# RMS scales of the mixing, memory, cross and expert norms applied behind the projections they feed

## The chip, the cores and the metric

The kernel runs as one program on one core of a Trainium2 chip. The metric is the device time of the whole program in microseconds (us). Engines are named as in the profile: PE multiplies matrices (PEld is its weight load), DVE is the vector engine, ACT the scalar engine, POOL the GpSimd engine, SP issues the DMA stream of weights.

## The reference, cut to what matters

Two blocks follow each other over 256 tokens of width 2048, stored transposed as x[128 partitions, 16 feature blocks k, 256 tokens]. The first ends with a final norm; the second has four norms whose outputs feed projections:

```
x = rmsnorm(x, final_norm_w)                       # "f1", end of the first block
h = rms_norm(x, g_mix);  proj = h @ w_in           # "mix": rq rk rv rg | dq dk dv | two gates
ret = retention(rotate(rq), rotate(rk), rv);  ret = ret * silu(rg)
dil = dilated_attention(rotary(dq), rotary(dk), dv)
x = x + (sigmoid(gate_ret)*(ret @ w_br_ret) + sigmoid(gate_dil)*(dil @ w_br_dil)) @ w_out
hc = rms_norm(x, g_cross);  memn = rms_norm(mem, g_mem)
x = x + memory_cross_attention(hc, memn, w_q, w_kv, w_o)
hf = rms_norm(x, g_ffn);  x = x + peer_ffn(hf, w_q, subkeys, u_tab, v_tab)
# rms_norm(x, g) = x * r * g, r = rsqrt(mean(x*x over features) + 1e-6), one r per token
```

Since r is one number per token, (x * g * r) @ W = ((x * g) @ W) * r.

## The kernel before, in words

**A tile of weights.** All weight matrices pass as tiles of 128 outputs by 2048 inputs through a ring of four buffers, loaded by SP's queue. For each half of a tile ACT rounds it into w_hi (line 1123), POOL subtracts to get the remainder w_lo (line 414), and PE multiplies: with w_hi 8 matmuls of 512 columns, the activations' rounded and remainder parts side by side (line 453), and with w_lo 8 of 256 columns (line 455). w_hi and w_lo have four half-tile slots, so ACT rounds a half once PE has finished the half four before it. DVE adds the two halves of the psum bank into the output tile (line 1545 in copy stages, 1980 where it is added to x). There are four banks, and four ring buffers. In index n of a stage's loop ACT thus works two tiles ahead of PE, POOL right behind ACT, and DVE when PE has finished tile n.

**Stages around the change**, in tiles: mlp (8 rounds of 8 up tiles, whose squared-relu result "hid" DVE splits at lines 2014 to 2018, and 8 down tiles, added to x at line 2025), ret 32, dil 36, gate 32, br_ret 8, br_dil 4 (merged with the sigmoid gates at lines 2185 to 2191), out2 16, kv 32 (16 for K, 16 for V), q 16, o 16, pq 16 (the experts' query, with key scores, and the top 16 of each half of the keys on DVE), then up and down tiles of the experts.

**A norm** stands between two stages. ACT squares x in quarters of four blocks into ntmp (line 1150), DVE sums them over the blocks in halves (line 1501, norm_part), PE sums over the partitions with two matmuls by ones (line 479), DVE forms mean+eps, ACT takes the root (line 1154), DVE the reciprocal, and then quarter by quarter DVE multiplies x by gain and r into ntmp (line 1537), ACT rounds to the high part (line 1162), DVE subtracts to get the low part (line 1528). The stage's first matmul waits for the first quarter. "f1" and "mix" run one after the other behind mlp, followed by the sine tables of the rotations (lines 2037 to 2047); "mem" runs behind br_dil, ahead of out2; "cross" behind the 16th kv tile; "ffn" behind o. The order on each engine is the order in which its program is written; semaphores join them.

## Time and profile before

| | |
|---|---|
| median of three runs | 4832.02 us (4825.33 to 4833.13) |
| span of the profiled execution | 4820.5 us |
| PE busy in the span | 4398.7 us (91%), 24530 matmuls |
| DVE / ACT / POOL busy | 2616.8 (54%) / 1728.6 (36%) / 3284.8 us (68%) |

The profile gives the profiled execution only as its span, the time from its first to its last instruction, without a time of its own; the three timed runs lie 4.8 to 12.6 us above that span, which is what lies around it. Read the table as: one engine, PE, is nearly always busy; what counts is where it is not.

### The profile page before, as it was taken

The page shows a single profiled execution, that of the slowest core. Times are in us where ns is not written, and L with a number is a line of the kernel's source. Part 1 is how long each engine was busy: PE and PEld are TensorE (multiplying, and loading weights), DVE is VectorE, ACT ScalarE, POOL GpSimd, SP SyncE. Part 2 cuts the span into 40 slices and gives each one's busy share as a digit, 9 for nine tenths or more (in the row PEclk, how much of TensorE's full clock was granted, in tenths as well). Part 3 has the DMA queues.
Part 4 walks back from the last instruction along what each step waited for, and adds up shares of the span by engine and source line. Part 5 has one row for each costly group of instructions (what it writes and reads, how often), then busy time and mean ns, then how long its engine had stood idle before and what let it go on. Part 6 is the DMA issues. An engine that isn't in the chain of part 4 may idle for free.

```text
span 4820.5 us, 66241 instructions
## 1 busy us (share of the span) xinstructions
PE 4398.7 (91%) x24530; PEld 3674.6 (76%) x24530; DVE 2616.8 (54%) x3800; ACT 1728.6 (36%) x1827; POOL 3284.8 (68%) x1304
## 2 busy tenths in 40 slices
PE   8898987899999969996988898898899999999998
PEld 1677754688888858885877786788888788888886
DVE  3325765355455553314163312496976886795794
ACT  1234422333333333432534432443333333333333
POOL 0357730678888847872867784677687788788776
PEclk9999979899999979997999999999999999999999
DMA  8356740345455534551544452444354454445443
GB/s 312 115 196 253 293 158 35 139 165 184 178 182 182 182 112 158 182 181 59 186 156 157 157 189 97 149 149 148 139 191 170 163 189 179 166 175 180 170 171 125
DMA packets 111085, 804.56 MB, mean 167 GB/s; under 512 B 12903, under 2 KB 13192, under 8 KB 14088
## 3 DMA queue, kind: packets, MB, share of 16 engines
q1 hardware_dynamic: 108720, 787.30, 45.0%
q10 hardware_dynamic: 2200, 14.90, 0.9%
q8 instruction: 122, 2.00, 0.2%
q14 instruction: 43, 0.35, 0.0%
HBM read 800.06 MB, written 2.10 MB: 166 GB/s over the span
## 4 chain that ended last, share of the span: by engine, by line
POOL 31%; PE 30%; issue 24%; DVE 4%; POOLq 1%; ACT 0%; DMA 0%; DVEq 0%; ACTq 0%
POOL w_lo L414 31%; PE psum L453 16%; PE psum L455 8%; PE psum L550 1%; DVE out_hl L2364 1%; PE psum L442 1%; PE psum L443 1%; PE psum L444 1%; PE psum L1071 1%; DVE out_hl L2362 1%; DVE hid L2360 0%; POOLq L411 0%; DVE mix_m L1789 0%; PE psum L1042 0%; DVE mix_t L1789 0%
## 5 line engine op out<-in xcount | busy, mean ns | idle before, releaser
L414 POOL TENSOR_TENSOR w_lo<-ring,w_hi 128x1024 fp32r<-128x1024 f32 x1240 | 3010.3, 2432 | 1389.2 <-ACT w_hi L1123 1388.7
L1123 ACT ACTIVATE w_hi<-ring 128x1024 fp32r<-128x1024 f32 x1240 | 1309.5, 1060 | 2173.5 <-PE psum L455 1939.6
L453 PE MATMUL psum<-hc_hl,w_hi 128*128 128x512 f32 x5440 | 1945.9, 401 | 109.5 <-DVE hc_hl L1528 43.7
L455 PE MATMUL psum<-hc_hl,w_lo 128*128 128x256 f32 x5440 | 1529.2, 281 | 0.0
L453 PEld LDWEIGHTS psum<-hc_hl,w_hi 128*128 128x128 f32 x5440 | 1029.6, 189 | 360.5 <-issue 71.6
L455 PEld LDWEIGHTS psum<-hc_hl,w_lo 128*128 128x128 f32 x5440 | 1036.2, 190 | 2.0 <-issue 1.9
L453 PE MATMUL psum<-out_hl,w_hi 128*128 128x512 f32 x2048 | 728.3, 400 | 26.3 <-issue 14.1
L455 PE MATMUL psum<-out_hl,w_lo 128*128 128x256 f32 x2048 | 577.1, 282 | 0.0
L453 PEld LDWEIGHTS psum<-out_hl,w_hi 128*128 128x128 f32 x2048 | 388.8, 190 | 123.3 <-issue 21.6
L455 PEld LDWEIGHTS psum<-out_hl,w_lo 128*128 128x128 f32 x2048 | 391.2, 191 | 0.0
L453 PE MATMUL psum<-hid_hl,w_hi 128*128 128x512 f32 x1024 | 360.9, 398 | 14.0 <-DVE hid_hl L2018 14.0
L429 POOL TENSOR_TENSOR ada_acc<-ada_acc,ada_row 128x2048 f32<-128x2048 f32 x56 | 256.2, 4575 | 70.3 <-ACT ada_row L1220 64.8
L455 PE MATMUL psum<-hid_hl,w_lo 128*128 128x256 f32 x1024 | 286.1, 279 | 0.0
L2025 DVE SCALAR_TENSOR_TENSOR x<-psum,mod,x 128x256 f32<-128x256 f32 x256 | 124.0, 484 | 227.3 <-PE psum L455 222.7
L550 PE MATMUL psum<-x,ring 128*128 128x256 f32 x1024 | 234.0, 389 | 8.4 <-DMA ring<-mixed 5.2
L453 PEld LDWEIGHTS psum<-hid_hl,w_hi 128*128 128x128 f32 x1024 | 192.3, 188 | 62.9 <-DVE hid_hl L2018 16.5
L550 PEld LDWEIGHTS psum<-x,ring 128*128 128x128 f32 x1024 | 197.6, 195 | 45.9 <-DMA ring<-mixed 7.9
L2372 DVE TENSOR_TENSOR x<-psum,x 128x256 f32<-128x256 f32 x256 | 107.9, 421 | 203.1 <-PE psum L455 196.9
L2364 DVE TENSOR_TENSOR out_hl<-hid,out_hl 128x256 fp32r<-128x256 f32 x128 | 197.9, 1546 | 4.4
L455 PEld LDWEIGHTS psum<-hid_hl,w_lo 128*128 128x128 f32 x1024 | 193.0, 188 | 0.0
L453 PE MATMUL psum<-mem_hl,w_hi 128*128 128x512 f32 x512 | 184.1, 404 | 9.6 <-POOL w_lo L414 9.6
L2016 DVE CAST hid_hl<-hid 128x256 fp32r<-128x256 f32 x64 | 159.8, 2497 | 2.2
(386 smaller groups left out, 5178.9 us busy)
## 6 DMA issues: line engine op xcount, KB each, us to landing
ring<-stream SPq DMA_DIRECT2D x652, 1024.0 KB, 4.8
ring<-mixed SPq DMA_DIRECT2D x96, 1024.0 KB, 6.5
x<-x ACTq DMA_DIRECT2D x2, 2048.0 KB, 11.2
ctx_raw<-ctx ACTq DMA_DIRECT2D x1, 2048.0 KB, 9.8
mem_raw<-mem ACTq DMA_DIRECT2D x1, 2048.0 KB, 7.6
out<-x SPq DMA_DIRECT2D x4, 512.0 KB, 2.6
filt_w<-filt_w ACTq DMA_DIRECT2D x1, 1024.0 KB, 11.0
dft<-dft ACTq DMA_DIRECT2D x1, 1024.0 KB, 12.7
```

Of the source, the lines that this page charges most:

```text
L414: pool.tensor_tensor(w_lo[:, slot], ring[:, s, k], w_hi[:, slot].bitcast(F32), ALU.subtract).then_inc(lo_ready, 1)
L429: pool.tensor_tensor(ada_acc[:, n % 2], ada_row[:, 0] if k == 1 else ada_acc[:, n % 2], ada_row[:, k % 2], ALU.add).then_inc(ada_done, 2 i ...
L442: pe.matmul(o, w_hi[:, slot, c], x_hi, start=start(c), stop=False)
L443: pe.matmul(o, w_hi[:, slot, c], x_lo, start=False, stop=False)
L453: pe.matmul(psum[:, b, :].rearrange("p (s t) -> p s t", s=2), w_hi[:, slot, c], x_hl, start=start(c), stop=False, skip_group_check=True)
L455: m = pe.matmul(psum[:, b, 0:T], w_lo[:, slot, c], x_hl[:, 0], start=False, stop=stop(c), skip_group_check=True)
L550: m = pe.matmul(psum[:, (3, 7)[i % 2], 0:T], ring[:, (3 * i) % RING, k], x[:, k], start=k == 0, stop=k == KC - 1)
L1123: act.activation(w_hi[:, 2 * (s % 2) + h], ring[:, s, k], ACT.Copy).then_inc(hi_ready, 1)
L2016: dve.tensor_copy(hid_hi[:, j], s).then_inc(dve_step, 1)
L2025: dve.scalar_tensor_tensor(x[:, d], psum[:, 4 + d % 4, s * T:s * T + T], mod[:, gate + d, 0:1], x[:, d], ALU.mult, ALU.add).then_inc(acc_f ...
L2364: dve.tensor_tensor(out_lo[:, j], hid[:], out_hi[:, j].bitcast(F32), ALU.subtract).then_inc(hid_ready, 1)
L2372: st.did(dve.tensor_tensor(x[:, d], psum[:, 4 + d % 4, 0:T], x[:, d], ALU.add))
```

## The change

It keeps every product and every norm, and moves where r is applied. The activations that a projection reads are now x * gain without r, rounded (ACT) and subtracted (DVE, `gained_low`) quarter by quarter inside the loop of the stage before. The squares and their sums run inside a tile loop too. r itself is made later and applied to what comes out: for ret to the rotation tables, to V on its way to natural order, and to the silu gate's input; the gate tiles are multiplied by it one by one (32); the K half of kv tile by tile (16), the V half at its turn; for cross in the scale of the softmax's Exp; for pq in that of the chosen scores' Exp. A row of r (r_row) serves where tokens lie along the free axis, a column (r_col) where they are partitions. The experts' up tiles still read the true h, which ACT and POOL make again during pq. The final norm of block one multiplies x during ret tiles 9 to 16. The sine tables are computed inside the last mlp round. Parts of the diff, cut to what the next section speaks of:

```diff
+            pool.wait_ge(xg_made, q + 1)
+            pool.tensor_tensor(ntmp[:, q % 2], ntmp[:, q % 2], r_row[:].unsqueeze(1).broadcast_to([P, 4, T]),
+                               ALU.mult).then_inc(xg_scaled, 1)
...
+            pool.tensor_tensor(h_lo[:, 4 * q:4 * q + 4], ntmp[:, q % 2], h_hi[:, 4 * q:4 * q + 4].bitcast(F32),
+                               ALU.subtract).then_inc(hn_lo, 1)
...
+        for n in range(8, KC):
+            g, s = FIRST["pq"] + n, n % RING
...
+            if n == 9:
+                pool.wait_ge(r_made, FFN_MADE)
+            if n in (10, 11, 13, 14):
+                ffn_scale((10, 11, 13, 14).index(n))
+            if n in (12, 13, 15):
+                ffn_low((12, 13, 15).index(n))
+        ffn_low(3)
+        split(2 * EXPERT_B, 2 * (FIRST["peer"] - SPLIT0))
...
+            def moving(k):
+                if after is not None and n == 0 and k % 4 == 0:
+                    pe.wait_ge(norm_lo, 4 * NS[after] + k // 4 + 1)
+                return hl[:, :, k]
+            for h in range(2):
+                half_wide(FIRST[name] + n, n % RING, h, lambda c: h == 0 and c == 0,
+                          lambda c: h == 1 and c == KC // 2 - 1, lambda c: n % RING, lambda c: moving(h * 8 + c))
...
+            if n == 2:
+                norm_pe("f1")
+            if n == 5:
+                norm_pe("mix", 5, mix_part)
+            if n == 7:
+                turn_root(1)
+            if n in (8, 9, 10, 11):
...
+        for n in range(KC):
+            tile("out2", n, h_hl)
+            if n == 12:
+                norm_pe("mem", column=True)
+        for n in range(KC):
+            tile("kv", n, mem_hl[:], "mem")
+            if n == 13:
+                norm_pe("cross", row=False, column=True)
...
+        def ffn_squares(q):
+            pe.wait_ge(norm_sq, 4 * NI["ffn"] + q + 1)
+            for k in range(4):
+                m = pe.matmul(psum[:, 7, 0:T], sq(ONES), ntmp[:, q % 2, k], start=q + k == 0, stop=q + k == 6)
+            m.then_inc(sq_used, 1)
...
+            act.wait_ge(acc_free, 4 + n_acc["peer"] - KC + 4 * q + 4)
+            gained(q, x, lambda k: final_mix[:, k:k + 1], h_hi)
...
+        act.dma_start(pos_i[:], a["pos"]).then_inc(s_aux, 16)
...
+                trig_sines(0)
+            if j == 9:
+                trig_sines(1)
+                act.wait_ge(r_made, FM_MADE)
+            if j in (12, 14):
+                mix_gained((j - 12) // 2)
+        split_at(FIRST["ret"])
+        mix_gained(2)
+        split_half(FIRST["ret"] + 1, 1, 0, True)
+        mix_gained(3)
+        split_half(FIRST["ret"] + 1, 1, 1)
+        square("f1", x, 0)
+        square("f1", x, 1)
+        def mix_square(q):
+            act.wait_ge(norm_half, 2 * NH["mix"] if q < 2 else 2 * NH["mix"] + 1)
+            for k in range(4):
+                m = act.activation(ntmp[:, q % 2, k], x[:, 4 * q + k], ACT.Square, scale=col("final1", 4 * q + k))
+            m.then_inc(norm_sq, 1)
...
+                square("f1", x, 3)
+            if n in (3, 4):
+                mix_square(2 * n - 6)
+                mix_square(2 * n - 5)
+            if n == 5:
+                root("f1")
+            if n == 8:
+                root("mix")
...
+            q = k // 4
+            m = act.activation(hi[:, k], src[:, k], ACT.Copy, scale=col(name, k))
+            if k % 4 == 3:
+                m.then_inc(norm_hi, 1)
+            if k % 8 == 0:
+                act.wait_ge(norm_half, 2 * NH[name] + k // 8)
+            m = act.activation(ntmp[:, q % 2, k % 4], src[:, k], ACT.Square)
+            if k % 4 == 3:
+                m.then_inc(norm_sq, 1)
+        for n in range(KC):
+            split_at(FIRST["out2"] + n)
+            if n == 2:
+                act.wait_ge(merged, 1)
+            if 2 <= n < 10:
...
+            split_at(FIRST["kv"] + n)
+            if n == 2:
+                act.wait_ge(bank_free, 4 + bank_of["kv"])
+            if 2 <= n < 10:
+                gained_squared("cross", x, h_hi, 2 * n - 4)
...
+        def ffn_again(q):
+            act.wait_ge(sq_used, 4)
+            if q >= 2:
+                act.wait_ge(hn_lo, q - 1)
+            for k in range(4):
+                m = act.activation(ntmp[:, q % 2, k], x[:, 4 * q + k], ACT.Copy, scale=col("ffn", 4 * q + k))
+            m.then_inc(xg_made, 1)
...
+        def ffn_high(q):
+            act.wait_ge(xg_scaled, q + 1)
+            act.activation(h_hi[:, 4 * q:4 * q + 4], ntmp[:, q % 2], ACT.Copy).then_inc(hn_hi, 1)
...
+        for n in range(KC):
+            split_at(FIRST["o"] + n)
+            if n in (6, 10, 14):
+                ffn_gained((n - 6) // 4)
+        split_at(FIRST["pq"])
+        split_half(FIRST["pq"] + 1, 1, 0, True)
+        ffn_gained(3)
+        split_half(FIRST["pq"] + 1, 1, 1)
...
+            if n < 6:
+                ffn_square(n - 2)
+            if n == 8:
+                root("ffn")
+            if n in (9, 10):
+                ffn_again(n - 9)
+            if n in (12, 13):
+                ffn_high(n - 12)
+            if n in (14, 15):
+                ffn_again(n - 12)
+            if n in (15, 16):
+                ffn_high(n - 13)
...
-        up_down_dve(FIRST["mlp"], bank_of["mlp"], 0, HID0, dict(STREAM)["mlp"] // 16, 5 * KC)
-        norm_dve("f1", x, lambda k: col("final1", k), plain=x)
-        dve.wait_ge(plain_done, 2 + 4)
-        norm_dve("mix", x, lambda k: col("mix", k))
...
+                m = dve.scalar_tensor_tensor(lo[:, k], src[:, k], gain(k), hi[:, k].bitcast(F32), ALU.mult, ALU.subtract)
+            m.then_inc(norm_lo, 1)
...
+                if d == 0:
+                    trig_cosine(0)
+                    trig_angle(1)
+                if d == 6:
+                    trig_cosine(1)
+                if d in (7, 11):
+                    dve.wait_ge(acc_free, 4 + acc0 + d + 1)
+                    mix_low((d - 7) // 4)
+                if d == 14:
+                    mix_low(2)
...
+        dve.wait_ge(acc_free, 4 + n_acc["peer"])
+        mix_low(3)
...
+        norm_half_sum("f1", 0)
         for n in range(RET_TILES):
             evict("ret", n, pr[:, n])
-            if n in (4, 5, 8, 9):
-                ret_v((n // 4 - 1) * 2 + n % 2)
+            if n == 0:
+                norm_half_sum("f1", 1)
+            if n == 2:
...
+                norm_half_sum("mix", 0, mix_part)
+            if n == 3:
+                dve.wait_ge(norm_rt, NI["f1"] + 1)
+                st.did(dve.reciprocal(nrstd[:], nrt[:]))
+                st.settle()
+                st.did(dve.tensor_tensor(nrt[:], nrstd[:], nrstd[:], ALU.mult))
+                norm_half_sum("mix", 1, mix_part)
+            if n == 5:
...
+                st.did(dve.scalar_tensor_tensor(nrt[:], psum[:, 5, 0:T], 1.0 / D, nrt[:], ALU.mult, ALU.mult))
+                st.settle()
+                dve.tensor_scalar(nrt[:], nrt[:], EPS, None, ALU.add).then_inc(norm_ms, 1)
...
+                st.did(dve.reciprocal(r_row[:], nrt[:]))
+                st.settle()
+                dve.tensor_tensor(r_row[:], r_row[:], nrstd[:], ALU.mult).then_inc(r_made, 1)
...
+            if n == 7:
+                st.settle()
+                st.did(dve.tensor_tensor(trig[:], trig[:], r_row[:].unsqueeze(1).broadcast_to([P, 4, T]), ALU.mult))
+                root_column(1, MIX)
...
+            if 9 <= n < 17:
+                for k in (2 * n - 18, 2 * n - 17):
+                    m = dve.scalar_tensor_tensor(x[:, k], x[:, k], col("final1", k), nrstd[:], ALU.mult, ALU.mult)
...
+        dve.wait_ge(bank_free, 4 + bank_of["dil"])
+        dve.tensor_tensor(pr[:, 24:32], pr[:, 24:32], r_row[:].unsqueeze(1).broadcast_to([P, 8, T]),
+                          ALU.mult).then_inc(pg_scaled, 1)
...
+                both(blk, j).then_inc(bank_free, 1)
+                dve.wait_ge(bank_free, i * RING + (4 + bank_of["gate"] + j + 1))
+                dve.tensor_tensor(blk, blk, r_row[:], ALU.mult).then_inc(pg_scaled, 1)
...
+            dve.wait_ge(half_done, 2 * (FIRST[name] + n) + 2)
+            st.did(dve.tensor_tensor(x[:, n], psum[:, n % RING, 0:T], x[:, n], ALU.add))
+            st.settle()
+            dve.tensor_tensor(x[:, n], psum[:, n % RING, T:], x[:, n], ALU.add).then_inc(bank_free, 1)
+        for n in range(KC):
+            added("out2", n)
+            if n in (3, 5, 7, 9):
+                gained_low("mem", (n - 3) // 2, mem_raw, lambda k: col("mem", k), mem_hi, mem_lo)
+            if n in (6, 10):
+                norm_half_sum("mem", (n - 6) // 4)
...
+        st.did(dve.reciprocal(r_row[:], nrt[:]))
...
+            st.did(dve.tensor_tensor(kv[:, n], kv[:, n], r_row[:], ALU.mult))
+            if n in (3, 5, 7, 9):
+                gained_low("cross", (n - 3) // 2, x, lambda k: col("cross", k), h_hi, h_lo)
+            if n in (6, 10):
+                norm_half_sum("cross", (n - 6) // 4)
+            if n == 13:
...
+        for n in range(KC):
+            added("o", n)
+            if n in (7, 11, 14):
+                ffn_low_part((n - 7) // 4 if n < 14 else 2)
         dve.wait_ge(bank_free, 4 + bank_of["pq"])
-        norm_dve("ffn", x, lambda k: col("ffn", k), summed=1)
+        ffn_low_part(3)
...
-            both(q_peer[:, n], n % RING).then_inc(bank_free, 1)
+            if n >= RING:
+                dve.wait_ge(p_sc, n - RING + 1)
+            both(q_peer[:, n % RING], n % RING).then_inc(bank_free, 1)
...
+                dve.wait_ge(sq_used, 4)
+                dve.tensor_scalar(nrt[:], psum[:, 7, 0:T], 1.0 / D, EPS, ALU.mult, ALU.add).then_inc(norm_ms, 1)
```

On ACT, between the last br_dil split and the first out2 tiles, before:

```order
L1150 ACTIVATE ntmp<-mem_raw 128x1024 x4
L1123 ACTIVATE w_hi<-ring 128x1024 x2
L1154 ACT_TABLE_LOAD
L1154 ACTIVATE nrt<-nrt 128x256
L1123 ACTIVATE w_hi<-ring 128x1024 x2
L1162 ACTIVATE mem_hl<-ntmp,cols 128x256 x16
L1123 ACTIVATE w_hi<-ring 128x1024 x4
```

The same piece of ACT after, from one out2 tile (L1187 is the split of a tile) to its two blocks of the memory norm:

```order
L1187 ACTIVATE w_hi<-ring 128x1024 x2
L1530 ACTIVATE mem_hl<-mem_raw,cols 128x256
L1535 ACTIVATE ntmp<-mem_raw 128x256
L1530 ACTIVATE mem_hl<-mem_raw,cols 128x256
L1535 ACTIVATE ntmp<-mem_raw 128x256
```

The norm's squares and high parts moved from a block of their own into the tile loop, two blocks of x behind each of eight splits (out2 tiles 2 to 9, in index n). The kv loop has the same form.

On DVE in the out2 loop, after, from tile 5 to tile 7 (L2486 and L2488 add a psum bank to x, L1687 is the half sum of the squares, L2220 the low parts):

```order
L2486 TENSOR_TENSOR x<-psum,x 128x256
L2488 TENSOR_TENSOR x<-psum,x 128x256
L2220 SCALAR_TENSOR_TENSOR mem_hl<-mem_raw,cols,mem_hl 128x256 x4
L2486 TENSOR_TENSOR x<-psum,x 128x256
L2488 TENSOR_TENSOR x<-psum,x 128x256
L1687 TENSOR_REDUCE norm_part<-ntmp 128x256
L2486 TENSOR_TENSOR x<-psum,x 128x256
L2488 TENSOR_TENSOR x<-psum,x 128x256
L2220 SCALAR_TENSOR_TENSOR mem_hl<-mem_raw,cols,mem_hl 128x256 x4
```

Each such row now stands behind the adds of a tile, while before all of them stood in front of the first.

On POOL in the pq stage, after (L461 splits half a tile, L430 multiplies four blocks by r, L437 makes their low parts):

```order
L461 TENSOR_TENSOR w_lo<-ring,w_hi 128x1024 x6
L430 TENSOR_TENSOR ntmp<-ntmp,r_row 128x1024
L461 TENSOR_TENSOR w_lo<-ring,w_hi 128x1024 x2
L430 TENSOR_TENSOR ntmp<-ntmp,r_row 128x1024
L461 TENSOR_TENSOR w_lo<-ring,w_hi 128x1024 x2
L437 TENSOR_TENSOR hc_hl<-ntmp,hc_hl 128x1024
L461 TENSOR_TENSOR w_lo<-ring,w_hi 128x1024 x2
L430 TENSOR_TENSOR ntmp<-ntmp,r_row 128x1024
L437 TENSOR_TENSOR hc_hl<-ntmp,hc_hl 128x1024
L461 TENSOR_TENSOR w_lo<-ring,w_hi 128x1024 x2
L430 TENSOR_TENSOR ntmp<-ntmp,r_row 128x1024
L461 TENSOR_TENSOR w_lo<-ring,w_hi 128x1024 x2
```

Before, nothing but splits stood there; eight instructions of another kind are new.

## Rows read from the trace of the kernel before

**Rows 1.** busy time, clock and DMA of the four norms' stretches
```profile
core 0: us, PE busy (x) PEld busy (x) DVE busy (x) ACT busy (x) POOL busy (x), PEclk, DMA share, GB/s
1703.30:1777.40 74.10, 27.45 (x110) 20.52 (x110) 51.89 (x82) 27.73 (x41) 20.46 (x9) 0.65 0.17 59
2526.50:2568.60 42.10, 25.18 (x107) 20.98 (x108) 30.58 (x43) 20.06 (x30) 21.66 (x9) 0.70 0.24 83
2731.50:2767.50 36.00, 22.48 (x108) 18.92 (x106) 27.08 (x39) 14.74 (x25) 19.54 (x9) 0.81 0.27 91
3082.60:3114.00 31.40, 10.31 (x42) 7.26 (x41) 26.03 (x38) 14.91 (x25) 11.97 (x5) 0.73 0.19 67
```

**Rows 2.** what PE waited for, 1703.3 to 1777.4 (us, times, longest)
```profile
PE psum L479 <- DVE norm_part L1501: 28.7, 4, 12.8
```

**Rows 3.** DVE in time, both norms behind mlp (start, us, [idle before])
```profile
1703.46 1.00 DVE L2025 SCALAR_TENSOR_TENSOR x<-psum,mod,x 128x256 f32<-128x256 f32 x2 [1.77 <-PE psum L455]
1706.53 3.59 DVE L1501 TENSOR_REDUCE norm_part<-ntmp 128x256 f32<-128x2048 f32 x1 [2.07 <-ACT ntmp L1150]
...
1776.70 0.69 DVE L1545 TENSOR_REDUCE pr<-psum 128x256 f32<-128x512 f32 x1 [9.32 <-PE psum L455]
1782.25 0.69 DVE L1545 TENSOR_REDUCE pr<-psum 128x256 f32<-128x512 f32 x1 [4.86 <-PE psum L455]
```

**Rows 4.** DVE in time, last eviction before and first behind mem, cross, ffn
```profile
2526.08 0.43 DVE L2191 TENSOR_TENSOR hc_hl<-mrg,hc_hl 128x256 fp32r<-128x256 f32 x1
...
2567.72 0.88 DVE L1980 TENSOR_TENSOR x<-psum,x 128x256 f32 x2 [7.03 <-PE psum L455]
...
2731.55 0.69 DVE L1545 TENSOR_REDUCE kv<-psum 128x256 f32<-128x512 f32 x1 [3.87 <-PE psum L455]
...
2766.76 0.69 DVE L1545 TENSOR_REDUCE kv<-psum 128x512 f32 x1 [6.54 <-PE psum L455]
...
3082.66 0.88 DVE L1980 TENSOR_TENSOR x<-psum,x 128x256 f32<-128x256 f32 x2 [3.46 <-PE psum L455]
...
3113.29 0.69 DVE L1545 TENSOR_REDUCE q_peer<-psum 128x256 f32<-128x512 f32 x1 [1.77 <-PE psum L455]
```

**Rows 5.** groups by line, 2600 to 2720, an undisturbed stretch of tiles
```profile
L414 POOL TENSOR_TENSOR w_lo<-ring,w_hi 128x1024 fp32r<-128x1024 f32 x43 | 103.1, 2397 | 18.5 <-ACT w_hi L1123 18.5
L1123 ACT ACTIVATE w_hi<-ring 128x1024 fp32r<-128x1024 f32 x42 | 44.6, 1062 | 74.1 <-PE psum L455 74.1
```

**Rows 6.** ACT in time, high parts of the mix norm
```profile
1744.80 3.30 ACT L1162 ACTIVATE hc_hl<-ntmp,cols 128x256 fp32r<-128x256 f32 x8 [5.06 <-DVE ntmp L1537]
```

**Rows 7.** DVE and POOL in time: mlp round, then br_dil with and without POOL
```profile
1619.31 2.51 DVE L2016 CAST hid_hl<-hid 128x256 fp32r<-128x256 f32 x1
1619.27 2.41 POOL L414 TENSOR_TENSOR w_lo<-ring,w_hi 128x1024 fp32r<-128x1024 f32 x1 [0.37 <-ACT w_hi L1123]
2501.39 2.21 DVE L2187 TENSOR_TENSOR mrg<-mrg,pg 128x256 f32<-128x256 f32 x1
2509.94 0.42 DVE L2187 TENSOR_TENSOR mrg<-mrg,pg 128x256 f32<-128x256 f32 x1
```

**Rows 8.** PE in time behind a long wait
```profile
2992.30 0.79 PE L453 MATMUL psum<-hc_hl,w_hi 128*128 128x512 f32 x1 [6.53 <-POOL w_lo L414]
```

**Rows 9.** busy time in the pq stage and in the first up tiles
```profile
3114.00:3206.00 92.00, 90.49 (x531) 78.46 (x530) 81.45 (x346) 35.22 (x44) 71.47 (x30) 1.00 0.45 164
3230.00:3300.00 70.00, 65.34 (x536) 64.33 (x535) 44.89 (x14) 32.31 (x38) 68.87 (x23) 1.00 0.46 165
```

**Rows 10.** what PE waited for, 3114 to 3314
```profile
PE psum L1010 <- DVE q_peer L1545: 7.4, 6, 5.9
```

**Rows 11.** from the page: groups by line (busy, mean ns | idle before, releaser)
```profile
L453 PE MATMUL psum<-hc_hl,w_hi 128*128 128x512 f32 x5440 | 1945.9, 401 | 109.5 <-DVE hc_hl L1528 43.7
...
L453 PE MATMUL psum<-hid_hl,w_hi 128*128 128x512 f32 x1024 | 360.9, 398 | 14.0 <-DVE hid_hl L2018 14.0
...
L550 PE MATMUL psum<-x,ring 128*128 128x256 f32 x1024 | 234.0, 389 | 8.4 <-DMA ring<-mixed 5.2
```

More of the change, by code:

```diff
@@ L1137, in split_stage, with square, root, gained @@
                     split_tile(i * RING + (g0 + s), i + g0 // RING, s)
+        def square(name, src, q):
+            if q >= 2:
+                act.wait_ge(norm_half, 2 * NH[name] + 1)
+            act.activation(ntmp[:, q % 2], src[:, 4 * q:4 * q + 4], ACT.Square).then_inc(norm_sq, 1)
+        def root(name):
+            act.wait_ge(norm_ms, NI[name] + 1)
+            act.activation(nrt[:], nrt[:], ACT.Sqrt).then_inc(norm_rt, 1)
+        def gained(q, src, gain, hi):
+            for k in range(4 * q, 4 * q + 4):
+                m = act.activation(hi[:, k], src[:, k], ACT.Copy, scale=gain(k))
+            m.then_inc(norm_hi, 1)
         def norm_act(name, src, shift=None, split=True, ready=None, ahead=None):
@@ L1147, in norm_act @@
                     act.wait_ge(*ready(q))
[L1148 to L1150 removed]
+                square(name, src, q)
             if ahead is not None:
@@ L1482, in _ @@
         act.wait_ge(p_cv, 1)
-        act.activation(chosen[:, 2], chosen[:, 2], ACT.Exp).then_inc(p_ge, 1)
+        for tb in range(2):
+            m = act.activation(chosen[:, 2, tb], chosen[:, 2, tb], ACT.Exp, scale=r_col[:, FFN, tb:tb + 1])
+        m.then_inc(p_ge, 1)
         up_act(0, EARLY, QUARTER - EARLY)
```

311 lines of the change are left out of this document (204 added, 107 removed).

## The prediction, made before the changed kernel ran

> **What bounds the kernel now.** I read the page first: PE is busy 91% of the span and its 512-column matmuls cost 0.401 us each, so what can be won is PE's idle time. The page puts 109.5 us of idle before one group of matmuls, most of it behind line 1528, the last step of a norm [rows 11]. Then I read busy time by stretches for the places where a norm stands between two stages: PE is busy only 27.45 of 74.1 us, 25.18 of 42.1, 22.48 of 36.0 and 10.31 of 31.4, with a granted clock of 0.65 to 0.81, while elsewhere it is 1.00 [rows 1, 9]. In the first stretch the waits name the half sums alone with 28.7 us [rows 2]: PE does not wait for one slow instruction but for a chain of ACT, DVE, PE, DVE, ACT, DVE.
>
> What each norm costs I take from the evictions on DVE, because one follows each finished tile. A tile takes 1782.25 − 1776.70 = 5.55 us. Behind mlp the last add to x starts at 1703.46 and the third ret tile is evicted at 1776.70: 73.24 − 3 × 5.55 = **56.6 us** lost to f1 and mix [rows 3]. In the same way [rows 4]: from the last merged block, 2526.08, to out2 tile 2, 2567.72, 41.64 − 16.65 = **25.0** (mem); from kv tile 15, 2731.55, to kv tile 18, 2766.76, 35.21 − 16.65 = **18.6** (cross); from o tile 15, 3082.66, to pq tile 0, 3113.29, 30.63 − 5.55 = **25.1** (ffn). In all 125.3 us. This is the most that the change can give back, lower clock behind the waits included; the matmuls of the projections are the same in number and shape.
>
> **The change part by part.** What is removed is the four waits, −125.3. What it puts in their place:
>
> *Mix.* The low parts of the first three quarters are written behind mlp's down tiles 3, 5 and 7. The fourth can't start before the last add to x: the adds 1.00 [rows 3], four high parts on ACT at 3.30/8 = 0.41 each [rows 6], four low parts on DVE at 0.42 to 2.4. PE has three quarters of a tile (4.2 us) to do meanwhile, but one half split must also be made between; I take 4. Further on, ACT and DVE now make the sums and roots in the tile loop. Each place where ACT waits for DVE holds up its next split: ACT's squares of the mixed x (index 5) behind DVE's half sum of 3.59 [rows 3], the two roots with their table loads, the sines in the last mlp round. PE's own small matmuls and the transposes of the root add a little. I take 5 for these and 3 for the 16 multiplications of x by the final gain, which stand in front of the retention's steps and share memory with POOL. Together 12, between 4 (all hidden but the last quarter) and 25 (each late by a POOL instruction).
>
> *Silu input and gates.* 32 multiplications by r, one per gate tile, 0.42 to 2.4 each beside 0.69 of eviction in 5.55 us: hidden. At the end br_ret waits for the last, and for one wide multiplication ahead of the silu: 3 (0 to 6).
>
> *Mem.* In br_dil DVE merges blocks at 2 instructions of 0.42 and a cast and a subtraction; while POOL splits, one of these took 2.21 [rows 7]. Before, POOL had nothing to do there, since out2's splits stood behind the norm. Now ACT and POOL split out2 tiles 0 and 1 during the merge: four POOL instructions, each of which may hold DVE by 2.21 − 0.42 = 1.8, so up to 7.2. PE waits for the merge at this point; I take 6.5. PE then starts behind a wait, and a 512-column matmul behind one of 6.53 us took 0.79 in place of 0.40 [rows 8, 11]: 1.3 more. Sum 7.8 (2 to 12).
>
> *The two stalls in out2 and kv.* In index 6 ACT wants to square block 8 into the buffer of the first half and waits for DVE's half sum. That sum stands behind the adds of tile 6, and these wait for PE to finish tile 6. ACT's split of tile 7 stands behind the square. So when PE has finished tile 6, tile 7 isn't split: adds or eviction 0.9, sum 3.59, one or two squares and a high part 1.2, half a split 1.06 on ACT, 2.40 on POOL [rows 3 to 5], that is 9.1, plus hand-overs, 9.4; and 1.2 for the clock. 10.6 for each of out2 and kv, **21.2**. The same doesn't come again in index 10, where ACT has no square left that waits. Bounds 0 and 30.
>
> *Cross otherwise.* Sixteen multiplications of K by r, the low parts, and the scale in Exp lie beside the tiles: 0 (0 to 6).
>
> *Ffn.* The fourth quarter as in mix, but with short adds: 0.8. PE sums the squares over partitions by itself, 16 matmuls of 256 f32 columns at 0.389 [rows 11]: 6.2, not hidden, for PE is the busy engine. POOL gets eight instructions over four blocks of x, the size of a half split: 8 × 2.40 = 19.2 in tiles 10 to 15 [rows 5]. In the pq stage it is busy 71.47 of 92.0 us [rows 9], that is 20.5 free over 15 tiles (30 splits), 1.37 each; over six tiles 8.2, so 11 are left over and POOL, which PE waits for, is late by them. ACT takes 8 rounds more, but is at 35.22 of 92.0. Behind pq the up tiles leave POOL no slack at all (68.87 of 70.0 [rows 9]), so that nothing is won back there, and a start without lead costs some 3. On the other side PE waited 5.9 at the end of pq for the last query tile, behind DVE's top-16 work [rows 10], and lost 1.2 to the clock behind it; with PE late, DVE has caught up. 0.8 + 6.2 + 11 + 3 − 7.1 = 13.9 (5 to 25).
>
> Sum: −125.3 + 12 + 3 + 7.8 + 21.2 + 13.9 = −67.4 us. On the span of 4820.5 that is 4753; the median lies 11.5 above the span, so **4765 us**.
>
> A rule speaks against the change. By the trace, an SBUF cast of DVE that started while POOL split took 2.51 us, to the end of POOL's instruction, and a product of two SBUF tiles 2.21 against 0.42 alone [rows 7]. The Trainium skill, "SBUF — State Buffer", section "Who interferes with whom", says that a VectorE instruction of the kind with two SBUF inputs and a GpSimd one that reads SBUF exclude each other, each keeping the shared port for its whole instruction. The trace agrees. By that rule every low part moved into a loop where POOL is at work costs more than where POOL rested; where DVE's lead covers it the sum stays at −67, at full price it is rival A.
>
> **The rivals.**
>
> A: *slower, by that exclusion.* The change puts 128 DVE instructions over two SBUF tiles into loops in which POOL splits: 64 low parts, 16 products of K, 32 of the gates, 16 of x. If each delays PE by a whole POOL instruction, 128 × 2.40 = 307, less 125.3, is +182: 5014 us. It decides from 125.3/128 = 1.0 us each. Against it: in mlp each of 64 up tiles has three such steps with POOL at work, and all PE idle behind them is 14.0 us [rows 11], 0.2 per tile. DVE has three banks of lead. 3%.
>
> B: *better: nearly everything hides.* If in index 6 ACT had enough lead, or POOL's extra work in pq fell into slack, 21 or 11 to 14 us of the sum go: 4744 for the first, about 4730 for both, and at the very best 4832 − 118 = 4714. For it: ACT idles 74 of 120 us in such a loop [rows 5]. Against it: the wait in index 6 is one of order, not of load. 20%.
>
> C: *less: moved waits cost more.* Bursts of four low parts beside POOL delay evictions by over three banks, POOL's lateness in pq runs on, and mix comes to its upper bound: 25 + 6 + 12 + 30 + 25 = 98 given back, −27: 4805. For it: all but the matmul terms rest on single instructions. 13%.
>
> D: *it doesn't shorten*, because the weights would bound PE in place of the norm. The DMA share is 0.17 to 0.27 in these stretches and 0.45 in pq [rows 1, 9], far from full. 1%.
>
> **How the numbers follow.** Forecast 63%, with its own range 4747 to 4782; A 3%, B 20%, C 13%, D 1%. Some 0.2% (10 us) is what a measurement of this kernel tells from no change. Within it lie D and the far end of C: 2%. Slower 3%. Faster 95%. For 8 in 10 I leave out the better half of B, the far half of C, A and D: 4735 to 4800.
>
> **What would show it.** Right: no stretch of DVE's evictions behind mlp, br_dil, kv tile 15 and o over 15 us; PE waiting about 10 us for POOL's split of tile 7 in out2 and in kv; PE waits for splits in pq tiles 11 to 15, about 11 us; the merge in br_dil with casts or products of over 2 us; last wait of pq gone. Wrong: no wait at tile 7 (B), a clock of 1.00 in pq throughout (B), or waits for evictions spread over every tile of the loops (A, C).

## The result, and the profile after

The changed kernel takes 4777.23 us (median of 4 runs, 4768.23 to 4782.63) against 4828.68 of the kernel before beside it (4 runs, 4824.33 to 4833.13): a ratio of 0.9902, 95% interval 0.9886 to 0.9919, some 51 us less by the medians and 47 by the ratio. The forecast was 4765, with a range of 4735 to 4800. The profiled execution has a span of 4773.0 us against 4820.5, 47.5 us less.

The head of the page after:

```profile
span 4773.0 us, 66080 instructions
...
PE 4410.6 (92%) x24574; PEld 3687.1 (77%) x24574; DVE 2683.7 (56%) x3793; ACT 1744.9 (37%) x1885; POOL 3311.5 (69%) x1312
```

Busy time of the stretches that answer to [rows 1], in the same columns: from the last add of mlp to the third ret tile; the merge in br_dil; from its end to the third out2 tile; from the last o tile to the first pq tile; and the pq stage, for [rows 9]:

```profile
1708.10:1728.80 20.70, 16.28 (x84) 13.86 (x83) 13.11 (x10) 14.79 (x22) 12.50 (x6) 0.92 0.32 110
2449.40:2492.90 43.50, 26.70 (x167) 24.97 (x165) 41.28 (x64) 8.40 (x8) 19.98 (x9) 0.80 0.34 117
2492.90:2511.40 18.50, 18.50 (x97) 16.25 (x98) 1.70 (x4) 8.13 (x13) 11.21 (x5) 0.91 0.21 74
3032.50:3041.90 9.40, 6.04 (x27) 5.00 (x26) 4.88 (x6) 4.29 (x7) 5.07 (x2) 0.85 0.36 115
3041.20:3160.60 119.40, 103.70 (x574) 90.21 (x573) 100.89 (x370) 52.86 (x72) 92.10 (x39) 0.94 0.38 132
```

The norms' holes are closed. Between the same starts as in [rows 3, 4], 73.2 us behind mlp became 21.2, 41.6 behind the merge 19.0, 35.2 behind kv tile 15 became 16.8, and 30.6 behind o 9.1. What came in their place stands in the waits of PE (us, times, longest), the view to read next. Its first row is of the whole execution, the second of the pq stage; of the seven waits in the first row one of 6.6, at the head of o, was there before with 6.5:

```profile
PE psum L492 <- POOL w_lo L424: 31.7, 7, 9.4
...
PE psum L1068 <- DVE q_peer L1731: 11.7, 4, 6.8
```

The account by stages comes from the evictions on DVE, as in the prediction, for both profiled executions (length of each stretch in us, from start to start; where a tile is added to x in two steps, the second; the kernels of the experiments are cut at the same evictions):

| stretch, up to | before | after | difference | forecast |
|---|---|---|---|---|
| first up tile of the last mlp round | 1618.1 | 1610.0 | -8.2 | 0 |
| last add of mlp | 85.9 | 98.2 | +12.3 | with ret |
| last ret tile | 257.2 | 209.4 | -47.8 | -44.6 with mlp |
| first merged block of br_dil | 530.6 | 531.8 | +1.2 | +3 |
| last merged block | 34.3 | 43.0 | +8.7 | +6.5 |
| last out2 tile | 115.5 | 105.2 | -10.3 | -13.1 |
| last kv tile | 198.6 | 190.8 | -7.8 | -8.0 |
| last o tile | 243.0 | 244.2 | +1.2 | 0 |
| first pq tile | 30.2 | 8.7 | -21.5 | -24.3 |
| last pq tile | 98.7 | 118.7 | +20.0 | +17.2 |
| end | 1608.5 | 1613.1 | +4.6 | -4.1 |

Two of these rows, the first and the last, hold no changed work that explains them. Up to the last mlp round the program is nearly the same, and the changed kernels below reached it between 1606.8 and 1619.4 us; in the stretch from the last pq tile to the end they took 1605.8 to 1616.8. So stretches of the same code differ by up to 13 us between executions. Single effects are read below from the length of their own stage, and the yardstick for each is how far kernels with the same code in it lie apart: the last mlp round took 95.0 to 98.4 us, the merge in br_dil 41.1 to 43.0, and pq 117.1 to 118.7. Each stage is read in one execution per kernel.

### The profile page after: what moved, and what is told of

Its sections match the earlier page's. It is cut to its first block, busy times and chain, and to the rows that moved or that the text cites. A ratio compares the mean times of both kernels' runs of the same rounds, so it can differ in the third digit from the quotient of the medians.

```text
span 4773.0 us, 66080 instructions
## 1 busy us (share of the span) xinstructions
PE 4410.6 (92%) x24574; PEld 3687.1 (77%) x24574; DVE 2683.7 (56%) x3793; ACT 1744.9 (37%) x1885; POOL 3311.5 (69%) x1312
## 4 chain that ended last, share of the span: by engine, by line
PE 33%; POOL 29%; issue 21%; DVE 5%; POOLq 0%; ACT 0%; DMA 0%; DVEq 0%; ACTq 0%
POOL w_lo L424 28%; PE psum L492 18%; PE psum L494 9%; PE psum L607 1%; DVE out_hl L2698 1%; PE psum L481 1%; PE psum L482 1%; PE psum L483 1%; PE psum L1132 1%; DVE out_hl L2696 1%; POOL w_lo L461 1%; DVE hid L2694 0%; DVE mix_m L1976 0%; POOLq L421 0%; PE psum L1103 0%
## 5 line engine op out<-in xcount | busy, mean ns | idle before, releaser
L424 POOL TENSOR_TENSOR w_lo<-ring,w_hi 128x1024 fp32r<-128x1024 f32 x1224 | 2979.9, 2440 | 1309.1 <-ACT w_hi L1187 1308.5
L1187 ACT ACTIVATE w_hi<-ring 128x1024 fp32r<-128x1024 f32 x1240 | 1309.9, 1060 | 2151.7 <-PE psum L494 1899.8
L492 PE MATMUL psum<-hc_hl,w_hi 128*128 128x512 f32 x5184 | 1853.0, 401 | 86.4 <-DVE hc_hl L2151 24.5
L494 PE MATMUL psum<-hc_hl,w_lo 128*128 128x256 f32 x5184 | 1455.0, 281 | 0.0
L492 PEld LDWEIGHTS psum<-hc_hl,w_hi 128*128 128x128 f32 x5184 | 980.3, 189 | 327.3 <-issue 47.9
L494 PEld LDWEIGHTS psum<-hc_hl,w_lo 128*128 128x128 f32 x5184 | 985.0, 190 | 2.0 <-issue 1.9
L492 PE MATMUL psum<-hid_hl,w_hi 128*128 128x512 f32 x1024 | 366.7, 402 | 20.4 <-DVE hid_hl L2205 12.3
L2212 DVE SCALAR_TENSOR_TENSOR x<-psum,mod,x 128x256 f32<-128x256 f32 x224 | 108.5, 484 | 201.7 <-PE psum L494 197.7
L481 PE MATMUL psum<-hc_hl,w_hi 128*128 128x256 f32 x512 | 150.8, 294 | 5.3 <-POOL w_lo L424 5.3
## 6 DMA issues: line engine op xcount, KB each, us to landing
filt_w<-filt_w ACTq DMA_DIRECT2D x1, 1024.0 KB, 10.6
```

Source lines behind the costliest of these rows:

```text
L424: pool.tensor_tensor(w_lo[:, slot], ring[:, s, k], w_hi[:, slot].bitcast(F32), ALU.subtract).then_inc(lo_ready, 1)
L481: pe.matmul(o, w_hi[:, slot, c], x_hi, start=start(c), stop=False)
L492: pe.matmul(psum[:, b, :].rearrange("p (s t) -> p s t", s=2), w_hi[:, slot, c], x_hl, start=start(c), stop=False, skip_group_check=True)
L494: m = pe.matmul(psum[:, b, 0:T], w_lo[:, slot, c], x_hl[:, 0], start=False, stop=stop(c), skip_group_check=True)
L1187: act.activation(w_hi[:, 2 * (s % 2) + h], ring[:, s, k], ACT.Copy).then_inc(hi_ready, 1)
L2212: dve.scalar_tensor_tensor(x[:, d], psum[:, 4 + d % 4, s * T:s * T + T], mod[:, gate + d, 0:1], x[:, d], ALU.mult, ALU.add).then_inc(acc_f ...
```

## The experiments

All are edits of the changed kernel. A ratio is to the kernel before, measured beside it, with its 95% interval. The medians of the kernel before lay between 4821.2 and 4828.7 us, so kernels of different groups are compared more safely by their ratios than by their medians.

### Where the half sum stands

```diff
-            if n in (6, 10):
-                norm_half_sum("mem", (n - 6) // 4)
+            if n in (4, 10):
+                norm_half_sum("mem", n // 10)
```

The same for "cross".

> From the changed kernel, DVE's first half sum of the squares stands behind tile 4 of out2 and of kv in place of tile 6. Theory (a wait of order): ACT's split of tile 7 no longer waits for PE to finish tile 6, the two steps between evictions of 17.1 and 17.0 us fall to the pitch of 5.6, PE's waits of 9.1 and 9.4 us for POOL's split go: 22 us less than the changed kernel's 4777, so 4755. Rival (a matter of load: DVE's low parts, held up by POOL, use up the lead): the stall only moves to another tile, less than 10 us are won, 4767 or more.

Measured 4750.95 us, ratio 0.9848 (0.9832 to 0.9864), 26 us under the changed kernel, whose interval (0.9886 to 0.9919) lies above. The stall in the changed kernel can be read link by link. DVE: tiles 6 and 7 of out2, with the half sum between; ACT: its square of block 8 waits for that sum, and the split of tile 7 stands behind it; POOL waits for ACT:

```profile
2533.59 0.42 DVE L2486 TENSOR_TENSOR x<-psum,x 128x256 f32<-128x256 f32 x1 [3.08 <-PE psum L494]
2534.05 0.42 DVE L2488 TENSOR_TENSOR x<-psum,x 128x256 f32<-128x256 f32 x1
2534.39 3.58 DVE L1687 TENSOR_REDUCE norm_part<-ntmp 128x256 f32<-128x2048 f32 x1
2550.71 0.42 DVE L2486 TENSOR_TENSOR x<-psum,x 128x256 f32<-128x256 f32 x1 [12.73 <-PE psum L494]
```

```profile
2538.01 0.42 ACT L1535 ACTIVATE ntmp<-mem_raw 128x256 f32<-128x256 f32 x1 [14.05 <-DVE norm_part L1687]
...
2539.04 1.99 ACT L1187 ACTIVATE w_hi<-ring 128x1024 fp32r<-128x1024 f32 x2
```

```profile
2540.15 14.31 POOL L424 TENSOR_TENSOR w_lo<-ring,w_hi 128x1024 fp32r<-128x1024 f32 x6 [14.11 <-ACT w_hi L1187]
```

With the sum behind tile 4, ACT waits 4.25 us at the same place, PE has no wait in out2, and one of 1.5 us in kv (its waits there, the whole answer):

```profile
PE psum L492 <- POOL w_lo L424: 1.5, 1, 1.5
```

out2 took 86.9 us from first to last tile in place of 97.2, kv 183.1 in place of 190.8: 18.0 together, under the 22 expected. The step into tile 7 fell from 17.1 to 5.7 us and from 17.0 to 7.4, 21.0 together; the other tiles took 3.0 more, with DVE's low parts held up by POOL. The medians differ by 8 us more than that; between the profiled executions, 7 us lie in the stretch behind pq, where nothing was changed. The wait was one of order, not of load.

### POOL's eight instructions in pq

```diff
-            pool.tensor_tensor(ntmp[:, q % 2], ntmp[:, q % 2], r_row[:]. ...
+            pool.tensor_tensor(ntmp[:, q % 2, :, 0:4], ntmp[:, q % 2, :, 0:4], ...
```

> From the changed kernel, POOL's eight instructions that make the experts' input again in pq work on 4 of the 256 tokens; the rest of that input is left out. Theory of the forecast (POOL is overloaded by 8 x 2.4 = 19.2 us, of which 11 show): 11 to 14 us less, 4764. Rival (pq is bound by DVE, which PE waits for 11.7 us there against 4.0 for POOL): at most 5 us less, 4772.

Measured 4775.71 us, ratio 0.9906 (0.9889 to 0.9922). The pq stage took 114.9 us in place of 118.7: 3.8 us, not 11 (2.2 against the shortest stage of the same code). POOL was no longer late (PE waited 0.5 us for it), and PE's waits for DVE's query tile grew from 11.7 to 13.6. The forecast's mechanism for pq falls.

### The expert norm as a block again

The norm stands between o and pq as before, without the squares on PE and the work on ACT and POOL in pq (some 60 lines back to their old form, in the new buffers).

> From the changed kernel, the expert norm alone goes back to what it was before: a block between o and pq, PE without the 16 matmuls over squares, POOL without the eight instructions. The forecast's sum (this part gives 11.2 us): 4788. Rival, read from the two traces (from the last q tile to the end the changed kernel is 6.0 us longer than the kernel before): 6 us less than the changed kernel, 4771.

Measured 4788.52 us, ratio 0.9922 (0.9904 to 0.9940); the intervals of this and of the changed kernel overlap, so the 11 us between the medians are not shown, though the median came where the forecast's sum had put it. The traces do not carry them: from the first o tile to the last pq tile it took 214.8 us, the changed kernel 213.7 (84.7 + 31.5 + 98.6 against 86.3 + 8.7 + 118.7). 7 of the 15 us between the spans lie in the memory attention, whose code is the same, at a granted clock of 0.78 against 0.88 (70 us each, this kernel first):

```profile
2885.00:2955.00 70.00, 48.45 (x185) 37.88 (x185) 20.56 (x33) 12.79 (x24) 5.05 (x3) 0.78 0.04 16
```

```profile
2877.00:2947.00 70.00, 48.64 (x215) 39.01 (x215) 21.29 (x35) 14.62 (x26) 11.72 (x5) 0.88 0.10 34
```

So this part of the change is worth about 1 us by its stages, in one execution of each; by the times alone 11 us cannot be ruled out. What it takes out of the hole between o and pq it gives back inside pq.

### out2's first splits behind the merge

```diff
         for n in range(KC):
-            split_at(FIRST["out2"] + n)
-            if n == 2:
+            if n == 0:
                 act.wait_ge(merged, 1)
+            split_at(FIRST["out2"] + n)
```

> From the changed kernel, ACT splits out2's tiles 0 and 1 only when the merge of br_dil is done, so that POOL rests in the merge's second half. Theory (DVE and POOL exclude each other: four merge steps took 2.35 to 2.59 us in place of 0.29 to 0.43): merge 8.5 us shorter, then 1.06 + 2.40 us of split ahead of PE: 5 us less, 4772. Rival (the merge is bound by PE or its own length): 3.5 us more, 4781.

Measured 4773.96 us, ratio 0.9893 (0.9877 to 0.9910), too little to tell from the changed kernel by time. By stage both terms came as the theory had them: the merge took 34.6 us in place of 43.0 (8.4 less; 6.5 against the shortest merge of the same code), and from its end to the first out2 tile 11.7 in place of 8.0 (3.7 more). In the changed kernel, one merge step that POOL held and what POOL did then:

```profile
2479.39 2.35 DVE L2474 CAST hc_hl<-mrg 128x256 fp32r<-128x256 f32 x1
2481.78 0.43 DVE L2476 TENSOR_TENSOR hc_hl<-mrg,hc_hl 128x256 fp32r<-128x256 f32 x1
```

```profile
2479.06 2.54 POOL L424 TENSOR_TENSOR w_lo<-ring,w_hi 128x1024 fp32r<-128x1024 f32 x1 [1.22 <-ACT w_hi L1187]
```

The cast starts inside POOL's instruction and ends 0.14 us behind it, at 2481.7; alone it takes 0.29. Eight instructions of POOL beside the merge held DVE eight times; with four of them gone it was held four times. The same shows all over the changed kernel's trace. From the last mlp round to the end of pq, 62 of DVE's 128x256 steps with two SBUF inputs started while POOL was within one of its instructions, 0.45 us or more ahead of its end. All 62 ended 0.28 or 0.29 us behind POOL's instruction. All 54 such steps that read psum for one input were done before POOL was.

### The second pair of sines

```diff
-            if j == 9:
+            if j == 11:
                 trig_sines(1)
```

> From the changed kernel, ACT takes the second pair of sines in the last mlp round behind its split 11 in place of 9. In the changed kernel ACT waited 13.0 us there for DVE's angles, which stand behind the first add of a down tile, and the last mlp round took 98.2 us against 85.3 before, where the forecast had some 1 us. Theory (a wait of order, like that of tile 7): the round is at least 8 us shorter, 4768 in all. Rival (the round is long because DVE's low parts and POOL exclude each other, 9.21 us for four low parts): less than 3 us, 4775.

Measured 4779.11 us, ratio 0.9911 (0.9894 to 0.9927): no gain in time. The last mlp round took 95.3 us in place of 98.2. ACT's wait was gone but for 3.9 us. But the same round took 95.0 and 95.3 us in two kernels further below that leave it as it is (four squares, and all of the expert norm's work shrunk), with the long wait still in it. ACT's waits in the round, this kernel first, then the one with four squares:

```profile
ACT trig L1424 <- DVE sin_a L2025: 3.9, 1, 3.9
```

```profile
ACT trig L1424 <- DVE sin_a L2025: 16.1, 2, 12.4
```

So no price of the wait is shown; it is at most 3 us, and the theory of 8 us falls.

### Squares and key scores on PE

Two kernels: PE sums 4 of 16 blocks; and the key scores go ahead of the squares.

```diff
-            for k in range(4):
+            for k in range(1):
                 m = pe.matmul(psum[:, 7, 0:T], sq(ONES), ntmp[:, q % 2, k], ...
```

> From the changed kernel, PE sums 4 of the 16 blocks of squares in pq; the other 12 matmuls are left out, the expert norm's scale is wrong by that. Forecast (PE is the busy engine, each of the 12 costs 0.389 us): the pq stage, 118.7 us from its first to its last eviction, is 4.7 us shorter. Rival (pq is bound by DVE, which comes late because the key scores stand behind the squares): at least as much, 5 to 8 us, since DVE's waits for scores, 7.5 us, go too. Either way near 4771; the stage's length tells.

> From the changed kernel, the key scores of a pq tile are issued ahead of the 4 matmuls over squares and of the transposes of the root, in place of behind them. Nothing is left out. Theory (pq is bound by DVE): DVE's waits for scores, 7.5 us, fall to some 2, the pq stage of 118.7 us is 4 to 6 us shorter, 4772 in all. Rival (PE's and POOL's work set the stage): no change, within 1 us.

Measured 4780.34 us (0.9919, 0.9903 to 0.9935) and 4774.73 us (0.9910, 0.9894 to 0.9927). The pq stage took 116.1 and 118.0 us in place of 118.7. Kernels with the pq stage unchanged took 117.1 to 118.7, so twelve squares are worth 1 to 2.6, less than they keep PE busy. That is 5.2 us and not the 4.7 of the expectation: the trace has two records for each of these matmuls, 0.38 us long and 0.215 us apart, so that one costs 0.43. The order of scores and squares shows no effect beyond that scatter: its theory falls, DVE's waits for scores stayed (7.8 us against 7.5).

### The low parts

```diff
-            for k in range(4 * q, 4 * q + 4):
-                m = dve.scalar_tensor_tensor(lo[:, k], src[:, k], gain(k), hi[:, k].bitcast(F32), ALU.mult, ALU.subtract)
-            m.then_inc(norm_lo, 1)
+            dve.tensor_scalar(lo[:, 4 * q:4 * q + 4], hi[:, 4 * q:4 * q + 4].bitcast(F32), 0.0, None,
+                              ALU.mult).then_inc(norm_lo, 1)
```

> From the changed kernel, the 64 low parts of mix, mem, cross and ffn (0.42 us each alone, 1.2 to 1.4 in the changed kernel) are replaced by 16 wide instructions that write zero, so the low parts of these activations are left out. Theory (they lie beside PE, behind three banks of lead, except the last quarter of mix and ffn): 8 us less at most, 4769. Rival A of the forecast (each costs PE a POOL instruction): 48 fewer at 2.4 us, 115 us less, 4662; half of that would still show.

Measured 4765.79 us, ratio 0.9882 (0.9861 to 0.9902), 11 us less than the changed kernel, at 0.24 us for each of the 48 instructions taken away. The intervals of the two overlap, but the stages agree. DVE's busy time fell by more than the count says: the 64 low parts took 1.2 to 1.4 us each on average, 82 us in all, and the 16 wide ones, with one SBUF input, 17 us. By stages: 5.1 in the last mlp round (1.9 against its shortest length with the same code), 3.5 ahead of the first pq tile (the last quarter, which PE waits for), 2.4 in pq, 2.1 in ret, nothing in out2 and kv. Rival A is far off: 1.0 us each was its point.

### The order in pq

```diff
-            if 3 <= n < 7:
-                ffn_squares(n - 3)
+            if 1 <= n < 5:
+                ffn_squares(n - 1)
```

and DVE's mean and reciprocal at n = 5 and 7, POOL's wait for the reciprocal at n = 10.

> From the changed kernel, three waits of order in pq are taken away, no work is left out: PE sums the squares behind tiles 1 to 4 in place of 3 to 6 (ACT waited 10.9 us for them between two splits), DVE makes mean and reciprocal behind tiles 5 and 7 in place of 6 and 8, and POOL waits for the reciprocal behind its splits of tile 10 in place of 9 (it waited 7.6 us). Theory (the pq stage of 118.7 us, 20 over the kernel before, is long because ACT's and POOL's waits hold up splits and then DVE): 8 to 14 us less in the stage, 4766 in all. Rival (the sum of added work sets it: 12 us more on DVE, 6 on PE): less than 3 us.

Measured 4776.51 us, ratio 0.9911 (0.9883 to 0.9938). ACT's wait of 10.9 us and POOL's of 7.6 were gone, and yet the stage took 115.7 us in place of 118.7. The theory of order falls here: PE, DVE and POOL are each over 75% busy in this stage, and with these waits away another appeared (POOL then waited 8.4 us for ACT's blocks).

### The sine tables at the head of out1

The tables' DVE instructions (21, where the expectation below counts 18) and ACT's four sines are issued ahead of out1's first eviction, the lines in the mlp round go.

> From the changed kernel, the sine tables are made at the head of out1, where DVE was idle for 8.8 us, in place of in the last mlp round; nothing is left out. Theory (the tables' 18 DVE instructions and two pairs of sines, between splits and hidden-layer steps, make the last mlp round 98.2 us long in place of 85.3): 8 to 10 us less there, some 1 us more in out1, 4769 in all. Rival (the low parts of the mix norm make the round long): less than 4 us.

Measured 4773.89 us, ratio 0.9910 (0.9891 to 0.9928). The last mlp round took 89.5 us in place of 98.2: 8.7 us, as the theory had it (5.5 against the shortest round of the same code). At out1 they cost next to nothing: from the last step before it to its last add it took 128.6 us, and 126.6 to 128.6 in the others. By time, 3 us less than the changed kernel, nothing is shown. What the tables did in the mlp round is worth reading. In this kernel, and in the one before, an up tile of the hidden layer costs DVE one hold-up by POOL, every time in the same step, and the next tile comes 5.55 us later:

```profile
1620.64 0.69 DVE L1733 TENSOR_REDUCE hid<-psum 128x256 f32<-128x512 f32 x1 [1.45 <-PE psum L494]
1621.37 0.42 DVE L2257 SCALAR_TENSOR_TENSOR hid<-hid 128x256 f32<-128x256 f32 x1
1621.83 2.45 DVE L2259 CAST hid_hl<-hid 128x256 fp32r<-128x256 f32 x1
1624.31 0.43 DVE L2261 TENSOR_TENSOR hid_hl<-hid,hid_hl 128x256 fp32r<-128x256 f32 x1
1626.19 0.69 DVE L1733 TENSOR_REDUCE hid<-psum 128x256 f32<-128x512 f32 x1 [1.45 <-PE psum L494]
```

In the changed kernel, in the three tiles behind the tables' steps, DVE no longer waits for PE, each of its three steps meets a POOL instruction, and the tile takes 7.5 us (one of the three):

```profile
1636.66 0.69 DVE L1731 TENSOR_REDUCE hid<-psum 128x256 f32<-128x512 f32 x1
1637.39 1.79 DVE L2249 SCALAR_TENSOR_TENSOR hid<-hid 128x256 f32<-128x256 f32 x1
1639.21 2.38 DVE L2251 CAST hid_hl<-hid 128x256 fp32r<-128x256 f32 x1
1641.63 2.51 DVE L2253 TENSOR_TENSOR hid_hl<-hid,hid_hl 128x256 fp32r<-128x256 f32 x1
1644.17 0.69 DVE L1731 TENSOR_REDUCE hid<-psum 128x256 f32<-128x512 f32 x1
```

The tables put DVE behind, and once behind it ran into a POOL instruction at each step and stayed behind for three tiles.

### All orders together

The half sums at 4, out2's splits behind the merge, the order in pq and the tables in out1, nothing left out.

> All of the above that take waits of order away, with nothing left out: half sums behind tile 4, out2's first splits behind the merge, the order in pq, and the tables in out1. If they add up: 17 us (out2 and kv, by their stages) + 5 (merge) + 11 (pq) + 8 (mlp) = 41 us less than the changed kernel, 4736. Rival (what is freed meets the next limit, DVE held up by POOL): half of it, 4756.

Measured 4741.38 us (4740.49 to 4755.15), ratio 0.9846 (0.9823 to 0.9869): the fastest of all, 36 us under the changed kernel. The ratio hardly differs from the first experiment's, 0.9848 (0.9832 to 0.9864), so by time the other orders show no sure gain on top of the half sums. By stages they do, and the stages add up: last mlp round -9.5, merge and start of out2 -4.3, out2 -11.5, kv -9.8, pq -3.6, together -38.7. That is nearly the sum expected, 41, with 4 in place of 11 from pq and 21 in place of 17 from out2 and kv.

### All of the expert norm's work in pq shrunk

```diff
-            act.activation(ntmp[:, q % 2], x[:, 4 * q:4 * q + 4], ACT.Square).then_inc(norm_sq, 1)
+            act.activation(ntmp[:, q % 2, :, 0:4], x[:, 4 * q:4 * q + 4, 0:4], ACT.Square).then_inc(norm_sq, 1)
```

and so on for ACT's other blocks, with the edits of the second and sixth experiment and the order of the ninth.

> From the changed kernel with the order in pq of e9_pq_order, everything that the expert norm adds to the pq stage on PE, ACT and POOL is shrunk, and what it would have computed is left out: PE sums 4 of 16 blocks of squares, ACT's squares, gained blocks and high parts and POOL's eight instructions work on 4 of the 256 tokens. DVE's three small steps stay. e9_pq_order's stage took 115.7 us, that of the kernel before 98.7; single shares taken away gave 3.8, 2.6 and 3.0 us. Theory (the stage is long by the sum of added work, as DVE and PE wait for each other by turns): 100 to 103 us. Rival (it is long by structure: four buffers for the queries, three banks for the scores, the order of waits): 110 us or more. The whole: 4763 or 4773.

Measured 4762.39 us, ratio 0.9866 (0.9846 to 0.9886). The stage took 105.5 us (columns as in [rows 1]):

```profile
3053.70:3159.20 105.50, 95.32 (x550) 83.01 (x549) 92.41 (x368) 42.70 (x72) 76.35 (x39) 0.97 0.45 156
```

10.2 us under the same order with the work in it, between the two expectations and nearer the theory. Of the 6.8 us over the kernel before, the four squares left (4 times 0.43, 1.7) and DVE's three steps (2.3) would account for 4.0; 2.8 stay open.

## Why the forecast was right, step by step

**The holes and most of their refill: right.** The size of the whole, -51 against -67, was missed by 16 us, within the range. There is luck in it: of the 47.5 us between the two profiled executions, 8.2 lie ahead of any changed work, and without them the forecast would have been missed by more. Cross and the two stalls were forecast nearly as they came: PE waited 9.1 and 9.4 us for POOL's split of tile 7, the steps from tile 6 to 7 took 17.1 and 17.0 us, so 11.6 and 11.4 over the pitch, against 10.6 each; cross came to -7.8 against -8.0. Of the first stall's 11.6 us, 9.1 are the wait, as forecast (9.4), and 2.5 come behind it, where the forecast had 1.2. The granted clock was at the lower of its two levels (0.51, 1.2 GHz) for the 5 us behind the wait:

```profile
2542.60:2547.60 5.00, 4.95 (x15) 4.28 (x16) 0.00 (x0) 3.14 (x6) 5.00 (x3) 0.51 0.28 85
```

Reading the order of three engines' programs, with durations from the trace, was enough for the stalls. Mem as a whole was not met: its two rows, the merge and out2, came to -1.6 together against -6.6, by 2.2 at the merge, 1.0 at the stall and some 2 on out2's other tiles, whose cause is open.

Three readings in the prediction were off without harm. Line 1528 ended 43.7 of the 109.5 us of idle time, the largest share but not most of it. The 11.5 us between span and median is no time around the span: each run's time is 1.7 to 2.1 us above its own span, and the rest is that the profiled execution was a fast one; the forecast of -67.4 doesn't depend on it. And no row gives the 118 in rival B's best case.

**The merge: right, a little small.** "Each of which may hold DVE by 1.8": it was 2.1 each, for the four of out2 8.4 by experiment against 6.5. POOL did have something to do there before, four splits of br_dil's own tiles that held DVE four times; the four new ones came on top.

**Mix: mis-sized.** The term was 12, measured 21.1 (56.6 less 35.5), inside its bounds of 4 to 25. Its first piece held: PE waited 4.4 us for the fourth quarter, against 4. The failed step is the sines in the last mlp round, which I had as one of several waits of ACT worth 5 together. The round grew by 12.3 us: 8.7 by the tables on DVE and what they set off (the experiment that moves them to out1), up to 5.1 by the low parts. The sum has no term for the tables' 21 instructions on DVE, nor for what a delay does to its meetings with POOL. The other 8.8 us of the 21.1 lie in ret and were not taken apart.

**Ffn: the step "POOL, which PE waits for, is late by 11" failed, and so did "with PE late, DVE has caught up".** The stage grew by 20.0 against 17.2, but that it came so near was luck: POOL's work alone was worth 3.8, and twelve squares up to 2.6. PE waited 4.0 us for POOL in pq and 11.7 for DVE, 6.8 of them at the end, where the forecast had none. DVE was the fuller engine already, and one of its lines tells how it was slowed: the sums of candidate scores, before and after, in the pq stage (count, busy, mean ns):

```profile
L2262 DVE TENSOR_TENSOR psc<-top_v 128x256 f32<-128x256 f32 x14 | 13.0, 968 | 0.2
```

```profile
L2585 DVE TENSOR_TENSOR psc<-top_v 128x256 f32<-128x256 f32 x14 | 22.8, 1664 | 0.2
```

9.8 us more for the same fourteen instructions. POOL held them up more often: 7 of the fourteen ended 0.28 us behind one of its instructions before, 11 after. It was not so much its new instructions as the new timing, for with those thinned the fourteen still took 20.1 us. With 2.3 us of new steps that is nearly all of DVE's 12.3 us more, 100.89 in the row above against 88.57 in the stage before:

```profile
3113.20:3212.60 99.40, 92.10 (x541) 79.73 (x539) 88.57 (x367) 37.26 (x46) 75.19 (x31) 0.99 0.45 163
```

Ahead of the stage the fourth quarter cost 3.6 us (9.1 less a tile of 5.55) where I had 0.8; without the low parts 3.5 of it were gone. The squares were priced a little low, at one record's length: 16 times 0.43 is 6.9, not 6.2. In all the part was worth 1 us by stages (the experiment with the block) where I had 11.

**Rivals.** A was right in its mechanism and wrong in its price: the low parts were worth 0.24 us each, where 1.0 would decide. DVE's steps were held at full length often, but PE paid for it in full only where it waited for DVE, as at the merge. The rule of the Trainium skill ("SBUF — State Buffer", "Who interferes with whom") that stands with it held in every row looked at: six merge steps with two SBUF inputs of 2.1 to 2.6 us that end 0.28 us behind POOL's instruction. The other two held were casts of 2.35 us with one SBUF input; they end 0.15 us behind it. B did not come about for order; most of what it promised came by changing the orders by hand (4741). C was on the right side of the forecast, but its price was not reached. D did not occur.

**The pieces after:** the waits at tile 7, the lengthened merge and no stretch of over 15 us between evictions behind mlp, br_dil, kv tile 15 and o came as the forecast said they would show, and the clock in pq was 0.94, not the 1.00 of B. Two signs failed: "PE waits for splits in pq tiles 11 to 15, about 11 us" came to 4.0, and "last wait of pq gone" to a wait of 6.8.

## What to carry to other kernels

When work of one engine is moved into a loop of another stage, write down for each wait which tile the waiting engine is at and which the awaited one, and keep the awaited step a tile earlier: two half sums moved two tiles ahead gave 18 us by their stages (26 by the medians) and left no work out. Free time on an engine is not cover if another engine's instructions can hold up its own, as POOL's splits did DVE's steps over SBUF tiles: once it is behind, it may meet that engine at each step and stay behind; put extra steps where the engine really waits, as at the head of out1. Where three engines of a stage are over 75% busy, don't price added work by one of them alone: pq got 6.9 us of new work on PE, 2.3 on DVE, 18 on ACT and 19.5 on POOL and grew by 20; single shares taken away gave at most 4 us, nearly all of them together 13.

## What was not expected of the hardware

One and the same DVE instruction, the cast of an up tile, took between 0.29 and 2.45 us, by where it met POOL alone, and the pattern held over many tiles: three steps of an up tile cost one hold-up in the steady state (5.55 us a tile) and three when DVE came late (7.5 us). Stretches with the same instructions differed by up to 13 us between executions; in one case 7 us in a stretch of 70 us with a granted clock of 0.78 against 0.88. The clock is not all of it: from the first to the last of the 16 q tiles, untouched by any edit and at a granted clock of 1.00, it took 83.2 us in nine of the fourteen profiled executions (the changed kernel's among them) and 84.8 in five (that of the kernel before among them).
